# An attention loop's copies and transposes in new places, and rows of the output products ahead of their chunks

## The reference

```python
def dilated_attention_mixer(h, w_in, q_gain, k_gain, w_out, positions):
    qkv = (h @ w_in).reshape(bsz, seq, A_N_GROUPS, 3, A_HEADS, A_HEAD_DIM)   # 3 groups, 16 heads of 64
    for g, (window, dilation) in enumerate(A_GROUPS):
        q = rope(rms_norm(qkv[:, :, g, 0], q_gain[g]), positions)
        k = rope(rms_norm(qkv[:, :, g, 1], k_gain[g]), positions)
        o, lse = dilated_window_attention(q, k, qkv[:, :, g, 2], window, dilation)
    alpha = jax.nn.softmax(jnp.stack(lses, axis=0), axis=0)
    out = jnp.sum(alpha[..., None] * jnp.stack(outs, axis=0), axis=0)
    return out.reshape(bsz, seq, A_WIDTH) @ w_out

def gla_mixer(h, w_in, ...):                 # 4 heads, keys of 128, values of 256, chunks of 64
    o = gla_chunk(q, k, v, log_af, strict=False) + flip(gla_chunk(flip(q), flip(k), flip(v), flip(log_ab), strict=True))
    o = rms_norm(o, out_gain).reshape(bsz, seq, B_V_WIDTH)
    return (o * jax.nn.silu(r)) @ w_out
```

## Time and profile before

| what | value |
|---|---|
| median of 3 runs | 1682.7 us (1679.94 to 1686.21) |
| the profiled execution | 1682.1 us, its span 1680.8 us |
| TensorE busy | 1614.7 us (96%), 10072 matmuls |
| VectorE busy | 1137.0 us (68%) |
| ScalarE busy | 818.6 us (49%) |
| GpSimd busy | 289.6 us (17%) |
| mean granted clock of TensorE | 0.991 |

### The profile page before, as it was taken

How to read it: one execution, slowest core, us unless ns; L and a number is a source line. 1 busy time by engine, 2 the same in 40 slices (tenths; PEclk the granted TensorE clock), 3 DMA queues, 4 the chain that set the end, 5 groups by cost and what they waited for, 6 DMA issues and landing times. The chain is left out here.

```text
span 1680.8 us, 25023 instructions
## 1 busy us (share of the span) xinstructions
PE 1614.7 (96%) x10072; PEld 1413.1 (84%) x10072; DVE 1137.0 (68%) x1539; ACT 818.6 (49%) x1057; POOL 289.6 (17%) x239
## 2 busy tenths in 40 slices
PE   8999999999999998999999999989999899999997
PEld 7878888799987886899988788669789888889986
DVE  5877675578886485676557664378887665678864
ACT  5436564454434463444434363465444554356643
POOL 4743240000010010000004300037645000000000
PEclk9999999999999999999999999999999999999999
DMA  7553341177786350787454322000000265556653
GB/s 262 190 173 128 124 134 67 51 267 250 237 315 226 103 192 32 245 274 229 151 181 154 101 58 97 0 19 1 1 1 1 76 189 181 183 162 193 190 182 114
DMA packets 155394, 240.96 MB, mean 143 GB/s; under 512 B 12272, under 2 KB 80624, under 8 KB 155152
## 3 DMA queue, kind: packets, MB, share of 16 engines
q1 hardware_dynamic: 141632, 208.69, 37.8%
q0 software_dynamic: 6816, 27.08, 4.3%
q10 hardware_dynamic: 6832, 3.59, 0.8%
HBM read 238.29 MB, written 1.05 MB: 142 GB/s over the span
## 5 line engine op out<-in xcount | busy, mean ns | idle before, releaser
L206 DVE TENSOR_TENSOR wlo<-raw,whi 128x2048 fp32r<-128x2048 f32 x200 | 462.9, 2328 | 167.7 <-ACT whi L190 166.4
L190 ACT ACTIVATE whi<-raw 128x2048 fp32r<-128x2048 f32 x198 | 372.8, 1888 | 256.5 <-PE ps L340 167.2
L338 PE MATMUL ps<-xf,whi 128*128 128x256 f32 x1056 | 294.9, 279 | 2.8 <-DVE xf L488 1.0
L339 PE MATMUL ps<-xf,whi 128*128 128x256 f32 x1056 | 293.9, 278 | 0.0
L340 PE MATMUL ps<-xf,wlo 128*128 128x256 f32 x1056 | 293.9, 278 | 0.0
L338 PE MATMUL ps<-whi,xs 128*128 128x512 f32 x672 | 267.8, 399 | 2.9 <-DVE xs L485 0.9
L340 PE MATMUL ps<-whi,xs 128*128 128x512 f32 x672 | 262.7, 391 | 0.0
L339 PE MATMUL ps<-wlo,xs 128*128 128x512 f32 x672 | 262.4, 390 | 0.0
L338 PEld LDWEIGHTS ps<-xf,whi 128*128 128x128 f32 x1056 | 199.0, 188 | 5.5 <-issue 5.4
L339 PEld LDWEIGHTS ps<-xf,whi 128*128 128x128 f32 x1056 | 199.0, 188 | 0.0
L340 PEld LDWEIGHTS ps<-xf,wlo 128*128 128x128 f32 x1056 | 198.8, 188 | 0.0
(11 more groups left out here) (377 smaller groups left out, 2628.4 us busy)
## 6 DMA issues: line engine op xcount, KB each, us to landing
raw<-in_ffn_w_gate_up SPq DMA_DIRECT2D x88, 512.0 KB, 5.0
raw<-in_a_w_in SPq DMA_DIRECT2D x72, 512.0 KB, 4.6
raw<-in_w_in SPq DMA_DIRECT2D x60, 512.0 KB, 4.4
wide<-in_w_mod POOLq DMA_DIRECT2D x24, 1024.0 KB, 7.4
raw<-in_w_up SPq DMA_DIRECT2D x44, 512.0 KB, 4.7
raw<-in_ffn_w_down SPq DMA_DIRECT2D x40, 512.0 KB, 4.6
raw<-in_b_w_in SPq DMA_DIRECT2D x24, 512.0 KB, 4.5
raw<-in_w_down SPq DMA_DIRECT2D x20, 512.0 KB, 4.0
```

Of the source, the lines that this page charges most:

```text
L190: self.hi_ok.inc(act.activation(self.whi[:, h % NHI, 0:nk, :], self.raw[:, h % NRAW, 0:nk, :], ACT.Copy))
L206: self.lo_ok.inc(dve.tensor_tensor(self.wlo[:, h % NRAW, 0:nk, :], self.raw[:, h % NRAW, 0:nk, :], self.whi[:, h % NHI, 0:nk, :].bitcast(F ...
L338: pe.matmul(o, ahi, bhi, start=start, stop=False)
L339: pe.matmul(o, ahi, blo, start=False, stop=False)
```

## The change

1. **Entry of the attention.** VectorE's first copies `left(0, 0)` now stand ahead of the three memsets, and the conversion of chunk 10's first half behind `left(0, 1)`.
2. **In the loop.** For all pairs but pair 4, `transposed(p + 1, 0..2)` and the two `left` stand earlier. Before: transposes at u % 4 = 1 (behind the values), 2 (behind the scores), 2 (behind the values). Now: 0 and 1 (behind the values) and 2 (behind the scores); the copies at u % 4 = 0 and 1 behind the result. Pair 4 stays as it was.
3. **End of the attention.** A new function `second_rows` makes rows of the first chunk's second half. Row 0 for tile 0 stands ahead of `values(30)`, row 1 ahead of `values(31)`, rows 0 and 1 for tile 1 ahead of the product, which makes only rows 2 and 3 of that half.
4. **Gated heads.** The product uses PSUM banks 0 and 1 in place of 4 and 5, all groups of the split bank 3. Three rows for tile 1 stand ahead of the last head's outputs; the other five behind them; `W.used` comes ahead of the last group; four `second_rows` behind it.

```diff
+    def second_rows(chunk, bank, t, seq, rows):
+        half = chunk[1]
+        wh, wl = W.of(half)
+        W.wait_pe(half)
+        for k in rows:
+            mm3(ps[:, bank, :], xh(HK + k, t * P, (t + 1) * P, seq), xl(HK + k, t * P, (t + 1) * P, seq), wh[:, k, :], wl[:, k, :], False, False)
...
+        def turns(p):
+            if p == N_P:
+                return []
+            if p == N_P // 2:
+                return [("values", 1), ("scores", 2), ("values", 2)]
+            return [("values", 0), ("values", 1), ("scores", 2)]
...
-                if u % 4 == 2 and p + 1 < N_P:
-                    transposed(p + 1, 1)
+                if ("scores", u % 4) in turns(p + 1):
+                    transposed(p + 1, turns(p + 1).index(("scores", u % 4)))
                 if first:
                     piece(j, u % 2, 0)
+                if u == N_U - 1:
+                    pe.wait_ge(xs_lo.sem, lo0 + 3)
+                    second_rows(out_chunks[0], 6, 0, 0, (0,))
                 if u:
                     values(u - 1)
-                if 1 <= u % 4 <= 2 and p + 1 < N_P:
-                    transposed(p + 1, 0 if u % 4 == 1 else 2)
+                for i in range(3):
+                    if turns(p + 1)[i:i + 1] == [("values", u % 4)]:
+                        transposed(p + 1, i)
...
+            second_rows(out_chunks[0], 6, 0, 0, (1,))
             values(N_U - 1)
...
             W.used.inc(first_rows(out_chunks[0], 7, 1, 0, (3,)))
+            second_rows(out_chunks[0], 7, 1, 0, range(2))
             prod_pe()
...
             dve.wait_ge(hr_out.sem, 6)
+            left(0, 0)
             for n, h in enumerate((0, 1, 1)):
                 i_ = dve.memset(qz[n][64 - 64 * h:128 - 64 * h, :, :], 0.0)
             aa_q0.inc(i_)
-            W.lo(chunks[N_CH + 1][0])
-            for i in range(2):
-                left(0, i)
-            W.lo(chunks[N_CH + 1][1])
+            left(0, 1)
+            for h in chunks[N_CH + 1]:
+                W.lo(h)
...
-                if u % 4 == 2 and p + 1 < N_P:
+                if u % 4 == 2 and p + 1 == N_P // 2:
                     left(p + 1, 1)
                 if u:
                     result(u - 1)
-                if u % 4 == 1 and p + 1 < N_P:
-                    left(p + 1, 0)
+                if p + 1 < N_P and u % 4 < 2 and u % 4 != (0 if p + 1 == N_P // 2 else 2):
+                    left(p + 1, u % 4 if p + 1 != N_P // 2 else 0)
...
-        split, lo0 = Split(lambda t, k: r[:, t, k * P:(k + 1) * P], 1, None, banks=(3, 3, 0, 0)), xs_lo.n
-        prod_pe, prod_act, prod_dve = add_product(out_chunks, 4, 2, 1, nxt_chunk, norm)
+        split, lo0 = Split(lambda t, k: r[:, t, k * P:(k + 1) * P], 1, None, banks=(3, 3, 3, 3)), xs_lo.n
+        prod_pe, prod_act, prod_dve = add_product(out_chunks, 0, 2, 1, nxt_chunk, norm, rows=range(2, HK))
...
                 pe.wait_ge(lb_at.sem, 2 * h + 2)
+                if h == GLA_HEADS - 1:
+                    first_rows(out_chunks[0], 1, 1, 1, range(HK - 1))
                 pe.wait_ge(lb_s.sem, h + 1)
...
-            first_rows(out_chunks[0], 5, 1, 1, range(HK))
-            first_rows(out_chunks[0], 4, 0, 1, range(HK - 1))
+            first_rows(out_chunks[0], 1, 1, 1, (HK - 1,))
+            W.used.inc(first_rows(out_chunks[0], 0, 0, 1, range(HK)))
             pe.wait_ge(lb_out.sem, 2 * GLA_HEADS)
             pe.wait_ge(xs_lo.sem, lo0 + 3)
             split.on_pe((GLA_HEADS - 1,))
-            W.used.inc(first_rows(out_chunks[0], 4, 0, 1, (HK - 1,)))
+            for t in range(TT):
+                second_rows(out_chunks[0], t, t, 1, range(2))
             prod_pe()
```

More of the change, by code:

```diff
@@ L353, in wait_xs, with chunk_tok @@
             xs_want[s] = 0
-    def chunk_tok(chunk, banks, tiles=(0, 1), parts=(0, 1), keep=False):
+    def chunk_tok(chunk, banks, tiles=(0, 1), parts=(0, 1), keep=False, rows=range(HK)):
         for s in parts:
@@ L362, in chunk_tok @@
             for b, t in zip(banks, tiles):
-                for k in range(HK):
+                for k in rows:
                     kk, t0 = s * HK + k, (t % 2) * P
@@ L622, in first_rows, with add_product @@
         return i_
-    def add_product(chunks, b0, b1, seq, nxt, norm, gate=None, tmp=None):
+    def second_rows(chunk, bank, t, seq, rows):
+        half = chunk[1]
+        wh, wl = W.of(half)
+        W.wait_pe(half)
+        for k in rows:
+            mm3(ps[:, bank, :], xh(HK + k, t * P, (t + 1) * P, seq), xl(HK + k, t * P, (t + 1) * P, seq), wh[:, k, :], wl[:, k, :], False, False)
+    def add_product(chunks, b0, b1, seq, nxt, norm, gate=None, tmp=None, rows=range(HK)):
         a0 = added.n
         def on_pe():
-            chunk_tok(chunks[0], (b0, b0 + 1), (2 * seq, 2 * seq + 1), (1,))
+            chunk_tok(chunks[0], (b0, b0 + 1), (2 * seq, 2 * seq + 1), (1,), rows=rows)
             last_tok(chunks[1], (b1, b1 + 1), seq)
@@ L1081, in layer_a @@
         lo0, turn_at = xs_lo.n, {18: 0, 20: 1, 25: 2}
-        prod_pe, prod_act, prod_dve = add_product(out_chunks, 6, 2, 0, nxt, norm)
+        prod_pe, prod_act, prod_dve = add_product(out_chunks, 6, 2, 0, nxt, norm, rows=range(2, HK))
         def x_of(j):
```

## The result

The kernel after takes 1673.64 us, median of 13 runs (1669.53 to 1681.5), the kernel before 1682.86 (1676.87 to 1688.06), 13 runs each side by side. The ratio is 0.9946, 95% interval 0.9933 to 0.9959. The forecast was 1672.8 in 1668 to 1678.

What follows compares the result with a forecast made beforehand. TensorE was taken as the bound, busy 1614.7 of 1680.8 us. From 1682.1, -4.2 - 1.4 - 2.6 - 2.15 + 0.5 = -9.85 gives 1672.2; with 0.6 for the median of before, 1672.8, range 1668 to 1678.

Steps and rivals of the forecast that it cites:

- Entry, -4.2: Entry of the attention: copies first remove TensorE's stop of 2.80 us and the clock's fall behind it, 1.41.
- Rival C: Entry gives half: second copies late at 125.6, or the clock falls all the same; 1674 to 1675 us, chance 0.12.
- First pair, -1.4: Attention loop: TensorE's wait of 1.23 us at 155.20 for copies goes, with a drain of 0.16.
- Pairs 5 to 7, -2.6: Attention from iteration 16 on: of about 5.0 us of waits, 0.6, 1.4 and 0.5 are left in the three pairs.
- Rival B: VectorE becomes the bound from iteration 16; the -2.6 becomes 0 to +1, about 1676 us; chance 0.17.
- End, -2.15: End of the attention: second_rows fill waits, 2.46 us less, but TensorE then waits for the second chunk's conversion.
- Gated heads, +0.5: Last gated head: stop grows from 1.9 to 3.5 us; -1.0 at full clock, +1.5 for a clock fall.
- Rival A: The gated heads keep the clock: 1.5 us less, 1671.3; chance 0.12.
- Rival D: Slower than before: the stop of 3.5 leaves TensorE at 1.2 GHz through the output product; up to 1695 us, chance 0.03.
- The rules of the page TensorE: Matmul & The Clock Gate: Matmuls stay in program order, else gated heads about -2.5 us; transposes count differently as activity, so entry could lose 1.4.
- The sum: Whole kernel: -4.2 - 1.4 - 2.6 - 2.15 + 0.5 = -9.85 us.

Runs made afterwards that it cites:

- The experiment: The changed kernel with only the part in question undone, read by its stretch: entry 14.12 us, pairs 5 to 7 (second half) 73.37, end 18.67, gated heads 33.38.

## Why the prediction was right, and where not

- **Entry, -4.2: right**, 4.16, with the steps as written: copies at 119.74 (119.8 forecast), second ones ended at 124.97 (124.8), no fall of the clock, scores at 128.68 (128.8). The experiment gives 4.4. Rival C is out.
- **First pair, -1.4: the wait right, a term put at nothing wrong.** The wait of 1.23 went, but 0.74 came back at pair 4. The prediction saw that in iterations 0 and 8 a copy of 1.4 now stands ahead of the rope's scaling, and put nothing for it, because TensorE's bank would be free in time. The bank was: TensorE has no wait there. But the rope behind the copy came later (the turn of 17.05), and TensorE met that at pair 4, at a wait for GpSimd that already stood in the trace of before and that the prediction did not name:

```profile
246.06 0.66 PE L1134 MATMUL ps<-cst,wide 128*128 128x128 f32 x4 [0.97 <-POOL wide L1035]
```

- **Pairs 5 to 7, -2.6: mis-sized.** It is 3.22, and 3.27 by the experiment. The estimate of what is left, 0.6 + 1.4 + 0.5 = 2.5, agrees with the 2.6 that I get for after by adding what lies between groups beyond their spacing (5.0 less 2.5 is 2.5; the 2.6 is 0.1 more than its own terms give). Too small was what stood there before: some 5.5 by the same count, not 5.0, and some 0.3 in still smaller gaps; both counts are estimates from starts. Rival B, VectorE as the bound, is out.
- **End, -2.15: right**, 2.05, with the wait for the second chunk's conversion, 0.23 (0.3 forecast); the experiment, 2.06.
- **Gated heads, +0.5: right**, 0.59, and 0.55 by the experiment: stop 3.54 (3.5), ended by xs, then a low clock that costs 1.6 (1.5), over the last of the three rows and half of the outputs. That the clock fell is luck in part, as the next point shows.
- **Rival A (the clock stays)** did not hold in after, but its chance of 0.12 was low. Seven traces here have the gated part of after and the same stop of 3.54. The gated head takes 32.36 in two of them, with no fall, 33.93 to 33.97 in three with one low stretch of 3.4, and 35.06 and 35.09 in two with 6.8. Against before's 33.34, which itself has one fall, this part thus lies between -1.0 and +1.8 from run to run. **Rival D**, the low clock through the product, was seen nowhere.
- **The rules of the page TensorE: Matmul & The Clock Gate** of the Trainium skill. Program order (Step-by-step: what each phase is for): the rows of after agree, the outputs stand at 647.73, behind the rows that waited to 644.98, although their states were done. Transposes that do not count in the same way (Part 4: PE-mode transpose): the entry has transposes every 3.2 and stayed at 1.00, so the 1.4 was not given back.
- **The sum** was 0.4 too large in its places: the first half gave 0.7 less than forecast and the second 0.6 more, which cancel for the most part. The stretches without the change added 1.2 to the span of after. That the median came within 0.9 of the forecast is luck to that extent: two errors of 0.7 and 0.6 of opposite sign, and falls of the clock in stretches that the change does not touch.

## What to carry to other kernels

Before work is put into an engine's wait, ask of every single instruction moved which operand it needs and when that is written: one row of three needed a later group and turned a gain of 4.7 us (33.34 to 28.62) into a loss of 0.6. When an instruction is put ahead of others on an engine that is not the bound, ask what else stands behind it and who meets that later: a copy of 1.4 that TensorE never waited for seems to have cost it 0.7 some 40 us on. And compare by stretches between rows that both kernels have: they repeat to 0.1 us where whole times differ by 4 us.

## What the runs showed that was not expected

- VectorE's conversion of 128x2048 and GpSimd's product of 128x512 do not share, they queue: 2.54 and 3.24 or 4.59 and 2.33, as the conversion starts 1.46 or 1.10 behind GpSimd's first product, of 1.27 (behind or ahead of the second); apart, 2.54 and 2.29.
- The same stop of TensorE comes with the low clock in one run and not in another: 1.91 in two traces of three, 3.54 in five of seven. The low level began inside the stop (as at 124.7 in before) or up to 1.4 us behind its end (as in after). The low stretches in these places were 3.4 or 6.8 long.
- A stretch of 0.97 idle, behind 2.74 of dummy products, brought no fall in the one trace that has it.
